# Ten products of a tile of zeros on TensorE, five ahead of and five behind the gain products, in front of the first transposes

## The chip, the cores and the metric
The kernel runs on one core of a Trainium2 chip. The metric is the device time in microseconds (us) of one execution. Before the change it is 1565.86 us, the median of three runs (1565.73 to 1567.34).

## The reference, cut to what matters
Two transformer blocks follow each other over 256 tokens of width 1024, all in float32. Only the head of the first one lies at the change:

```python
h = rmsnorm(x, norm1_w)          # x * rsqrt(mean(x*x) + eps) * gain
proj = h @ w_in                  # 1024 columns of x into retention, MoBA and gate columns
rq, rk, rv, rg, mq, mk, mv, ga, gb = split(proj)
# retention and MoBA attention, their output products, a residual,
# a gated feed-forward; then the second block of two layers (FoX and MLA
# attention, four feed-forwards, per-layer gates) on the result
```

Everything behind `proj` is the same before and after the change, and so is what is computed in the head.

## The kernel before, in words
The tokens lie in two tiles of 128 (t = 0 and 1). Each weight matrix is loaded in pieces of 128 x 2048 ("units") by SyncE's queue into a ring `w_raw`. ScalarE makes a rounded copy `w_hi` of each unit (line 1132), and VectorE, or GpSimd for some units, the rest `w_lo = w_raw - w_hi` (lines 1561 and 480). The left operand is split in the same way into `xTh` and `xTl`, and a product of float32 precision is three products of the reduced type: high by high, high by low, low by high.

The head runs as follows. GpSimd sets constants: the epsilons, `ones` (a row of 128 ones, line 462), and 128 columns of zeros in `mask[:, 0:P]` (line 463), which raises `zeros_set` to 1. ScalarE's queue loads the gain row `norm1_w` and the identity. TensorE's first work is at line 831: two products of `ones` (one row by 128 columns) by the gain row (one row by 512 columns) which spread the gain over 128 partitions into banks 2 and 3. ScalarE sums the squares of tile 0 of x, VectorE takes the reciprocal (line 1650) and multiplies x by it and by the gain from the banks (line 1661, two halves of 512 columns). TensorE transposes the result in eight products with the identity, four for each half (line 521, called from `to_xT`). ScalarE copies the two banks of transposes out as `xTh` (line 1141), and VectorE makes `xTl` (line 1601). Between the transposes of tile 0 and tile 1, TensorE runs the first products of stage `rq0`: `xTh` by `w_hi` (line 570), by `w_lo` (line 576) and `xTl` by `w_hi` (line 583), for unit 0 and then for half of unit 1.

Each engine has its instructions in a written order. ScalarE's is: squares of tile 0, `w_hi` of unit 0, the two copies of transposes of tile 0, squares of tile 1, `w_hi` of unit 1. VectorE's is: reciprocal and normalization of tile 0, `w_lo` of unit 0, the two `xTl` of tile 0, reciprocal and normalization of tile 1, `w_lo` of unit 1. TensorE's queue waits on semaphores that the others raise.

Of the kernel before, what the change touches and what calls it, by code (L numbers as in the profile page):

```python
# [30 lines left out]
P = 128  # L31
# [155 lines left out]
def build(nc, dram, marks):  # L187
# [23 lines left out]
    with ExitStack() as ctx:  # L211
        def sb(name, cols, dt=F32):
            return ctx.enter_context(nc.sbuf_tensor(name, [P, cols], dt))
# [3 lines left out]
        def sem(name):  # L217
            sems[name] = ctx.enter_context(nc.semaphore(name))
            return sems[name]
# [19 lines left out]
        mask = sb("mask", 2 * P)[:, :]  # L239
# [85 lines left out]
        bank = [low[:, b] for b in range(4)]  # L325
# [14 lines left out]
        zeros_set, rope_q_loaded = sem("zeros_set"), sem("rope_q_loaded")  # L340
# [10 lines left out]
        def mark(name, *label):  # L351

            counts[name] += 1
            if label:
                assert label not in found, label
                found[label] = (name, counts[name])
            return 1
# [34 lines left out]
        def _(sp):  # L392
# [5 lines left out]
            def load(u):  # L398
                _, kt, n, halves = units[u]
                slot = w_raw[u % RING][:, 0:kt * n].rearrange("p (k n) -> p k n", k=kt)  # L400
                if u >= RING:
                    sp.wait_ge(w_lo_done[u % RING], u // RING)
                for (k0, k1), (n0, n1), src in halves:
                    sp.dma_start(slot[:, k0:k1, n0:n1], src).then_inc(w_loaded[u % RING], 16)
# [78 lines left out]
        def gb_count(site):  # L483

            return 16 * (site + 1) if site < 2 else 32 * site
# [21 lines left out]
        def _(pe):  # L507
# [100 lines left out]
            def tile_steps(stage, banks, **kw):  # L608


                c = Chunk(stage, banks, **kw)

                def early():
                    c.run(0, tiles=(0,))
                    c.run(1, tiles=(0,), part=0)

                return [early, lambda: c.run(1, tiles=(0,), part=1), lambda: c.run(0, 1, tiles=(1,))]
# [206 lines left out]
                                   [(j * P, src[:, 2 * i + t, j * P:(j + 1) * P]) for j in range(4)])  # L824


            pe.wait_ge(ones_set, 1)
            pe.wait_ge(gb_loaded, gb_count(0))
            for q in range(2):
                take(2 + q, ("norm", 0, 1, 1))  # L830
                mm = pe.matmul(bank[2 + q], ones, gain_row[:, q * CH:(q + 1) * CH], start=True, stop=True)
            mm.then_inc(pe_done, mark("pe_done", "gain0"))
            pe.wait_ge(ident_loaded, 16)
            rq = tile_steps("rq0", (0, 1), ready=0)
            to_xT(0, normed, b0=4, between=rq[0])
# [1344 lines left out]
```

## Time and profile before
| | |
|---|---|
| median of three runs | 1565.86 us |
| the profiled execution's own time | 1565.49 us |
| its span, first to last instruction | 1563.5 us |
| mean granted TensorE clock | 0.994 of full speed |
| TensorE matmul busy | 1517.2 us, 97% of the span, 8444 instructions |
| TensorE weight load busy | 1315.5 us, 84% |
| VectorE busy | 933.9 us, 60% |
| ScalarE busy | 783.6 us, 50% |
| GpSimd busy | 182.8 us, 12% |

PE is TensorE, PEld its weight loads, DVE VectorE, ACT ScalarE, POOL GpSimd and SP SyncE. A product of full float32 operands stands as two MATMUL records and two weight loads; a transpose and a product of the reduced type as one. A record's duration holds the drain of the pipeline as well, so that back-to-back records overlap: the pace is read from start to start. "Idle before" in square brackets names what ended the wait.

### The profile page before, as it was taken

What the parts mean: (1) busy time and instruction counts of PE and PEld (TensorE: products, weight loads), DVE (VectorE), ACT (ScalarE), POOL (GpSimd) and SP (SyncE); (2) the same over time, 40 slices, a digit from 0 to 9 for tenths busy, and PEclk for the clock granted to TensorE, in tenths of its full rate; (3) what the DMA queues carried; (4) which work ended last, traced back from release to release, by engine and by line L of the source; (5) the groups of instructions that cost most, each with busy time, mean ns of one, the idle gap of its engine ahead of it and who ended that gap; (6) DMA issues with size and microseconds to landing.
All of it is one profiled execution on the core that took longest, in us unless ns stands there. A gap on an engine that the chain in (4) does not pass through costs nothing.

```text
span 1563.5 us, 22063 instructions
## 1 busy us (share of the span) xinstructions
PE 1517.2 (97%) x8444; PEld 1315.5 (84%) x8444; DVE 933.9 (60%) x1214; ACT 783.6 (50%) x935; POOL 182.8 (12%) x54
## 2 busy tenths in 40 slices
PE   8999999999999999899999999899999999999997
PEld 6888888888888888798888888788888887888885
DVE  7475465666656667214666667766666355666667
ACT  5436444444444444655454446554446554544455
POOL 0014211000010001350100002100005441100001
PEclk9999999999999999999999999999999999999999
DMA  8444345655565554532555555565554334555552
GB/s 311 168 141 170 140 162 187 216 192 188 183 193 189 189 190 159 163 134 86 175 199 188 190 193 197 171 202 190 191 192 161 103 112 164 172 199 188 188 201 81
DMA packets 186861, 274.35 MB, mean 175 GB/s; under 512 B 9953, under 2 KB 137057, under 8 KB 186722
## 3 DMA queue, kind: packets, MB, share of 16 engines
q1 hardware_dynamic: 182848, 261.72, 50.2%
q10 hardware_dynamic: 3954, 11.80, 2.3%
q8 instruction: 42, 0.69, 0.2%
q14 instruction: 17, 0.14, 0.0%
HBM read 272.44 MB, written 1.05 MB: 175 GB/s over the span
## 4 chain that ended last, share of the span: by engine, by line
PE 83%; DVE 9%; ACT 4%; issue 1%; DMA 1%; POOL 0%; ACTq 0%; SPq 0%; DVEq 0%
PE bank L652 22%; PE bank L654 12%; PE bank L525 6%; PE bank L527 6%; PE bank L526 6%; PE acc L525 6%; PE acc L526 6%; PE acc L527 6%; DVE w_lo L1561 3%; PE acc L787 2%; ACT w_hi L1132 2%; PE acc L521 2%; PE bank L576 1%; PE bank L570 1%; PE bank L583 1%
## 5 line engine op out<-in xcount | busy, mean ns | idle before, releaser
L1561 DVE TENSOR_TENSOR w_lo<-w_raw,w_hi 128x2048 fp32r<-128x2048 f32 (+2 forms) x210 | 477.1, 2276 | 181.6 <-ACT w_hi L1210 121.6
L652 PE MATMUL bank<-xT,w_hi 128*128 128x512 f32 x1520 | 380.2, 392 | 2.0 <-DVE hid L1705 1.2
L480 POOL TENSOR_TENSOR w_lo<-w_raw,w_hi 128x2048 fp32r<-128x2048 f32 (+2 forms) x42 | 176.7, 4211 | 1345.6 <-ACT w_hi L1132 1345.6
L652 PEld LDWEIGHTS bank<-xT,w_hi 128*128 128x128 f32 x1520 | 276.1, 189 | 53.9 <-DVE hid L1705 1.6
L1210 ACT ACTIVATE w_hi<-w_raw 128x2048 fp32r<-128x2048 f32 x145 | 276.5, 1907 | 0.0
L654 PEld LDWEIGHTS bank<-xT,w_lo 128*128 128x128 f32 x1520 | 207.4, 190 | 14.8
L654 PE MATMUL bank<-xT,w_lo 128*128 128x256 f32 x1520 | 211.9, 282 | 0.0
L1132 ACT ACTIVATE w_hi<-w_raw 128x2048 fp32r<-128x2048 f32 (+4 forms) x107 | 191.8, 1817 | 27.9 <-DMA w_raw<-in_w_in 7.8
L525 PE MATMUL acc<-w_hi,hTh 128*128 128x512 f32 x400 | 156.2, 391 | 0.0
L526 PE MATMUL acc<-w_lo,hTh 128*128 128x512 f32 x400 | 156.2, 391 | 0.0
L527 PE MATMUL acc<-w_hi,hTl 128*128 128x512 f32 x400 | 155.6, 389 | 0.0
L525 PE MATMUL bank<-w_hi,xT 128*128 128x512 f32 x352 | 139.7, 397 | 2.0 <-DVE w_lo L1561 1.7
L527 PE MATMUL bank<-w_hi,xT 128*128 128x512 f32 x352 | 137.3, 390 | 0.0
L526 PE MATMUL bank<-w_lo,xT 128*128 128x512 f32 x352 | 137.0, 389 | 0.0
L1220 ACT ACTIVATE squares<-bank 128x512 f32<-128x512 f32 x50 | 29.8, 597 | 140.5 <-PE bank L654 140.5
L1779 DVE CUSTOM_DVE_ANT_0 arena<-acc,mask 128x128 f32<-128x128 f32 x80 | 25.4, 355 | 121.0 <-PE acc L787 121.0
L1231 ACT ACTIVATE hTh<-hid 128x512 fp32r<-128x512 f32 x45 | 28.5, 632 | 136.2 <-PE acc L527 136.2
L527 PEld LDWEIGHTS acc<-w_hi,hTl 128*128 128x128 f32 x400 | 75.1, 188 | 16.0
L525 PEld LDWEIGHTS acc<-w_hi,hTh 128*128 128x128 f32 x400 | 75.3, 188 | 14.3
L526 PEld LDWEIGHTS acc<-w_lo,hTh 128*128 128x128 f32 x400 | 75.3, 188 | 13.7
L1220 ACT ACTIVATE tanh<-bank 128x512 f32<-128x512 f32 x45 | 26.8, 596 | 106.7 <-PE bank L654 106.7
L525 PEld LDWEIGHTS bank<-w_hi,xT 128*128 128x128 f32 x352 | 66.1, 188 | 15.9 <-DVE w_lo L1561 1.5
(221 smaller groups left out, 2145.9 us busy)
## 6 DMA issues: line engine op xcount, KB each, us to landing
w_raw<-in_ffn_w_in SPq DMA_DIRECT2D x176, 512.0 KB, 4.4
w_raw<-in_ffn_w_out SPq DMA_DIRECT2D x88, 512.0 KB, 4.2
w_raw<-in_w_in SPq DMA_DIRECT2D x52, 512.0 KB, 4.8
w_raw<-in_fox_w_in SPq DMA_DIRECT2D x24, 512.0 KB, 4.5
w_raw<-in_w_ffn_gate SPq DMA_DIRECT2D x22, 512.0 KB, 4.7
w_raw<-in_w_ffn_up SPq DMA_DIRECT2D x22, 512.0 KB, 4.5
w_raw<-in_w_ffn_down SPq DMA_DIRECT2D x22, 512.0 KB, 3.9
w_raw<-in_ple_w_gate SPq DMA_DIRECT2D x16, 512.0 KB, 4.1
```

The costliest lines, as they stand in the source:

```text
L480: pool.tensor_tensor(w_lo[s][:, 0:cols], w_raw[u % RING][:, 0:cols], w_hi[s][:, 0:cols].bitcast(F32), ALU.subtract).then_inc(w_lo_done[u % ...
L521: mm = pe.matmul(bank[b][:, c:c + P], src, ident, is_transpose=True, start=True, stop=True)
L525: pe.matmul(out, ah, bh, start=first, stop=False)
L526: pe.matmul(out, ah, bl, start=False, stop=False)
L527: return pe.matmul(out, al, bh, start=False, stop=last)
L652: pe.matmul(out, wh[:, k, m], both, start=k == 0, stop=False)
L654: mm = pe.matmul(out[:, S:], wl[:, k, m], xTh[:, k], start=False, stop=k == KD - 1)
L787: mm = pe.matmul(out if n is None else out.rearrange("p (a n) -> p a n", a=n), a, b_, start=j == 0, stop=j == len(terms) - 1)
L1132: nc.scalar.activation(w_hi[slots[u]][:, 0:cols], w_raw[u % RING][:, 0:cols], ACT.Copy)\
L1210: nc.scalar.activation(w_hi[slots[u]][:, :], w_raw[u % RING][:, :], ACT.Copy).then_inc(w_hi_done, 1)
L1220: nc.scalar.activation(dst.rearrange("p (m n) -> p m n", m=2), low[:, b:b + 2, S:], ACT.Copy)\
L1561: nc.vector.tensor_tensor(w_lo[s][:, 0:cols], w_raw[u % RING][:, 0:cols], w_hi[s][:, 0:cols].bitcast(F32), ALU.subtract).then_inc(w_lo_don ...
```

## The change
Five products of the zero tile by itself, 128 x 128 by 128 columns in float32, are issued on TensorE's queue ahead of the gain products, and five behind them, ahead of the wait for the identity. They write 128 columns of bank 0, which nothing reads before `rq0` starts that bank anew. The first batch waits for `zeros_set`. Nothing else changes.

```diff
+            pe.wait_ge(zeros_set, 1)
+            zeros = mask[:, 0:P]
+            for _ in range(5):
+                pe.matmul(bank[0][:, 0:P], zeros, zeros, start=True, stop=True)
             pe.wait_ge(ones_set, 1)
             pe.wait_ge(gb_loaded, gb_count(0))
             for q in range(2):
                 take(2 + q, ("norm", 0, 1, 1))
                 mm = pe.matmul(bank[2 + q], ones, gain_row[:, q * CH:(q + 1) * CH], start=True, stop=True)
             mm.then_inc(pe_done, mark("pe_done", "gain0"))
+            for _ in range(5):
+                pe.matmul(bank[0][:, 0:P], zeros, zeros, start=True, stop=True)
             pe.wait_ge(ident_loaded, 16)
             rq = tile_steps("rq0", (0, 1), ready=0)
             to_xT(0, normed, b0=4, between=rq[0])
```

## Rows read from the trace of the kernel before
**Rows 1.** The page: busy time by engine, and the chain's shares.
```profile
PE 1517.2 (97%) x8444; PEld 1315.5 (84%) x8444; DVE 933.9 (60%) x1214; ACT 783.6 (50%) x935; POOL 182.8 (12%) x54
PE 83%; DVE 9%; ACT 4%; issue 1%; DMA 1%; POOL 0%; ACTq 0%; SPq 0%; DVEq 0%
```
**Rows 2.** Chain that ended last, 0 to 60 us: start, us, what.
```profile
1.67 5.77 DMA w_raw<-in_w_in
...
9.41 0.51 DVE w_lo L1561
...
11.62 1.28 DVE xT L1601 x2
13.01 1.41 DVE arena L1661 x2
14.41 2.21 DVE w_lo L1561
16.67 0.73 PE bank L576 x2
```
**Rows 3.** Timeline, 0 to 30 us, TensorE: start, us, engine, line, count [idle before].
```profile
3.28 3.75 PE L831 MATMUL bank<-gb,arena 1*128 1x512 f32 x4 [3.28 <-DMA gb<-in_norm_w]
...
7.96 1.94 PE L521 MATMUL acc<-ident,arena 128*128 128x128 f32 x8 [0.93 <-DVE arena L1661]
...
10.01 2.04 PE L570 MATMUL bank<-w_hi,xT 128*128 128x512 f32 x4
...
11.85 1.62 PE L576 MATMUL bank<-w_lo,xT 128*128 128x512 f32 x4
...
13.31 1.09 PE L583 MATMUL bank<-w_hi,xT 128*128 128x512 f32 x4
...
14.69 0.61 PE L583 MATMUL bank<-w_hi,xT 128*128 128x512 f32 x2
...
16.67 0.73 PE L576 MATMUL bank<-w_lo,xT 128*128 128x512 f32 x2 [1.36 <-DVE w_lo L1561]
...
17.24 1.04 PE L521 MATMUL acc<-ident,arena 128*128 128x128 f32 x8
```
**Rows 4.** Timeline of TensorE alone, two narrow windows, 12.9 to 13.5 us.
```profile
12.35 1.12 PE L576 MATMUL bank<-w_lo,xT 128*128 128x512 f32 x3
...
12.78 0.70 PE L576 MATMUL bank<-w_lo,xT 128*128 128x512 f32 x2
```
**Rows 5.** Line 521 in 7 to 12 us: durations in ns, first and last start.
```profile
L521 PE MATMUL acc<-ident,arena x8: 421/421/447, 8.0 to 9.5; 128*128 128x128 f32 x8
```
**Rows 6.** Timeline of GpSimd, ScalarE and VectorE in the head.
```profile
0.96 0.20 POOL L463 MEMSET mask<- 128x128 f32 x1
...
1.71 1.28 ACT L1141 ACT_TABLE_LOAD   x1 [1.71 <-PEq L2169]
...
7.07 1.41 DVE L1661 SCALAR_TENSOR_TENSOR arena<-x,rstd,bank 128x512 f32<-128x512 f32 x2 [0.85 <-PE bank L831]
7.47 1.91 ACT L1132 ACTIVATE w_hi<-w_raw 128x2048 fp32r<-128x2048 f32 x1 [1.52 <-DMA w_raw<-in_w_in]
...
9.28 1.25 ACT L1141 ACTIVATE xT<-acc 128x512 fp32r<-128x512 f32 x2
...
12.01 1.90 ACT L1132 ACTIVATE w_hi<-w_raw 128x2048 fp32r<-128x2048 f32 x1
...
14.33 2.29 DVE L1561 TENSOR_TENSOR w_lo<-w_raw,w_hi 128x2048 fp32r<-128x2048 f32 x1
```
**Rows 7.** Timeline of TensorE, 1290 to 1305 us: full float32 products of 128 columns.
```profile
1290.64 0.39 PE L800 MATMUL acc<-arena 128*128 128x128 f32 x2
1290.86 0.39 PE L801 MATMUL acc<-arena 128*128 128x128 f32 x2
```
**Rows 8.** Windows of 13 us: busy time by engine, then granted clock, DMA share, GB/s.
```profile
975.00:988.00 13.00, 8.02 (x36) 6.72 (x35) 10.53 (x20) 10.73 (x16) 2.93 (x1) 0.78 0.25 81
...
1547.00:1560.00 13.00, 6.40 (x29) 4.96 (x27) 10.14 (x22) 8.59 (x13) 0.00 (x0) 0.84 0.10 40
```

## The prediction
> **What bounds the kernel now.** I read the page first, then the chain of waits for the first 60 us, then the timeline of the head engine by engine, and last the granted clock in windows over the whole span. The page shows TensorE busy for 97% of the span and carrying 83% of the chain [rows 1]. So what shortens TensorE's work shortens the kernel, wherever TensorE is what the end waits for. The change touches TensorE alone, and only before its first transposes, so the question is whether TensorE is on the chain there. The chain says it isn't. It starts with the load of the first weight unit, runs through VectorE's `w_lo` of unit 0, the two `xTl`, the normalization of tile 1 and `w_lo` of unit 1, and enters TensorE for good only at 16.67 us, at line 576 [rows 2]. In the timeline the reader sees the same from TensorE's side: it is done with all earlier work at 15.30 us (14.69 + 0.61) and idles 1.36 us until `w_lo` of unit 1 comes [rows 3].
>
> Next comes TensorE's own pace before that wait. Eight transposes take 1.94 us at 7.96 and 1.04 us at 17.24 [rows 3]. From start to start that is 0.22 us ((1.94 - 0.42) / 7, with the 0.42 us that one record lasts [rows 5]) against 0.11. A product of 512 columns starts 0.43 us after the one before (12.35 to 12.78) where later four of them take 1.09 us in all, 0.23 us each [rows 3, 4]. So the first stretch runs at half pace, the lower of the two levels of 1.2 and 2.4 GHz, although the granted-clock column has no entry below 1.00 there. Behind 12.78 two products start before the one of 13.31, so one gap was about 0.30 and the next 0.23 [rows 4]: the clock rose near 12.9 us. That is 9.6 us after TensorE's first product at 3.28, and 4.9 us after the end of its last long pause at 7.96 [rows 3].
>
> **The change, part by part.** Nothing is removed or moved; 10 products are added, which are 20 matmul records and 20 weight loads.
>
> Price of one: a full float32 product of 128 by 128 by 128 columns is in the trace of before, in the late attention. Two follow each other at 1290.64 and 1290.86, 0.22 us apart at the upper clock [rows 7]. At the lower level, where transposes and wide products both showed twice the pace, it is 0.45. Five are 1.1 us at the upper level and 2.2 at the lower. No reason excludes that a product beside a busy array costs less, but the floor is nothing; the far end is the pace of the gain products, 3.75 / 4 = 0.94 us a record [rows 3], which would make 9.4 us of five (10 records). Those stream four times the columns, so the row of equal shape is the nearest, and I take 0.45.
>
> Batch one: the zeros are there at 1.16 us (0.96 + 0.20), and another engine's start was released at 1.71 by TensorE's queue [rows 6], so TensorE can start between 1.16 and 1.7. Five cold products end at 3.4 to 3.9. TensorE was idle until 3.28, when the gain row came [rows 3]; so 2.1 us or less of the 2.2 are covered, and the gain products start 0.1 to 0.6 us late. The wait added for the zeros has the gain products queued behind it, but it is met 1.6 us or more before their row arrives.
>
> Batch two: 7.03 (3.28 + 3.75) to 7.96 was a pause of 0.93 us, in which VectorE normalized the first half [rows 3, 6]. VectorE's 7.07 hangs on the last gain product. What the five cost depends on the clock.
> (a) Clock up before or during it. In the kernel before, the clock rose 4.9 us after the end of the last pause. With the first batch in place there is no pause from 1.2 to 1.7 us on, which puts the rise at 6.1 to 6.6. By then some three of the four gain records are done; the rest goes at double pace, and the gains end near 6.9 to 7.2. Five products at 0.22 end near 8.0 to 8.3, the normalized half is there 0.9 us after the gains, 7.8 to 8.1, and the transposes start at 8.0 to 8.3. Four of them take 0.33 + 0.27 us at the upper level, so the first bank is ready at 8.6 to 8.9. ScalarE isn't: it is in `w_hi` of unit 0 until 9.38 and copies the bank at 9.28 by the record [rows 6], held by the load that landed at 7.44 [rows 2]. So nothing behind ScalarE moves.
> (b) Clock up only after it. The gains end at 7.1 to 7.6, the batch at 9.4 to 9.9, and the first bank is ready 1.08 us (3 x 0.22 + 0.42) later, at 10.5 to 11.0. ScalarE's copy moves by 1.2 to 1.7 us.
>
> What lies between the copy and the end of the head: ScalarE's order takes the copies, the squares of tile 1 and `w_hi` of unit 1, ending at 13.91 (12.01 + 1.90). VectorE takes that unit up at 14.33 [rows 6], when its own chain is through; so ScalarE has 0.4 us of slack. VectorE itself is without a gap from 9.41 to 16.62 [rows 2, 6], and its only other tie to the transposes is `xTl` at 11.62, which needs copies that end at 10.53, 1.1 us of slack. So (a) costs 0.0, and (b) costs 1.2 - 0.4 to 1.7 - 0.4, 0.8 to 1.3 us. From 16.67 on TensorE runs what it ran before, at the pace it had before.
>
> What becomes faster in (a) is real but lies in front of a wait: eight transposes save 0.9 us and the wide products from 10.01 to 12.9 save half of 2.9 us, 1.4; together 2.3 us on TensorE. They turn the idle of 1.36 us before 16.67 into one of some 2.5 to 3.6. That is the whole effect I expect to see. The cover is the DMA, ScalarE, VectorE chain; if that were shorter by x, up to x of the gain would show.
>
> The sum against the profiled execution (1565.49 us, 2.0 of it around the span of 1563.5): 0.0 in case (a). The runs' median lies 0.4 us above that execution, so the forecast stands at 1565.9 us.
>
> One rule of the Trainium skill speaks for more. The page TensorE: Matmul & The Clock Gate, section "Why this matters for your kernels", advises keeping the array busy, so that the products run at the upper level. The trace agrees that the first products here run at half pace. By that rule alone the sum would be -2.3 us, the gain at TensorE; the rows of the chain say that TensorE isn't waited for there, and that is the third case below. The same page, section "Part 4: PE-mode transpose", says that transposes don't count as work for the clock. By it the rise near 12.9 would go back to the 2.9 us of wide products from 10.01 alone, and ordinary products put in front would raise the clock sooner still: an argument for (a) and against (b). The trace can't separate the two.
>
> **The rivals.**
> First, (b), the clock doesn't rise by then: the added work doesn't do what it would have to. For it: 3.75 us of gain products without a pause didn't raise the clock, and if the time from the first product counts (9.6 us), the rise comes at 10.8 to 11.3, behind the batch. Also the gain products use one row of the array and may count for little. Against it: the stretch without a pause grows from 3.75 to over 6 us. Time: +0.8 to +1.3, 1566.7 to 1567.2. It decides once the first bank of transposes is ready later than 9.28 + 0.4; this is the case on the slow side.
> Second, TensorE does bound the head: the wait at 16.67 is really for its own earlier work, and 2.3 us come back, 1563.6 us. For it: 97% busy. Against it: the named releaser, VectorE, ended at 16.62, and TensorE was empty at 15.30.
> Third, a shift elsewhere. Late in the kernel there are stretches at a lower clock, 0.78 of 13 us at 975 and 0.84 at 1547 [rows 8]. At half pace the first is 13 x 0.22 x 2 = 5.7 us long and costs up to 2.9 us, the second up to 2.1. When such a stretch begins or ends may move with the moment at which TensorE began its work; 1 to 3 us either way, 1563 to 1569. Against it: the three runs of before lie within 1.6 us.
>
> **How the numbers follow.** (a) has 0.56, (b) 0.25, the gain in the head 0.05, a shift elsewhere 0.14. The predicted time is that of (a), 1565.9 us. The range is 1563.9 to 1568.2: above, it takes in (b) with the 1.5 us by which the highest run of before stands over the median, nearly; below, most of the shifts, and it stops just short of the second rival. The bound of 0.2% is 3.1 us, about what a measurement of this kernel can tell from no change. None of the first three cases reaches it; only a third of the shifts, or products priced at the far end, would. So 0.03 for faster, 0.92 for the same, 0.05 for slower.
>
> **What would show it.** In the profile after: 20 records of full float32 products, 10 from about 1.2 to 1.7 us on, 10 behind the gain products; the pace of the second batch (0.22 or 0.45) tells (a) from (b). Then eight transposes at 7.96 or later in 1.0 to 1.1 us rather than 1.94; ScalarE's first copy still at 9.28; VectorE's `w_lo` of unit 1 still at 14.33 to 14.41; TensorE's wait before line 576 longer than 1.36 us and still ending at 16.67. The forecast is wrong if that product starts over 0.3 us earlier or later, or if the windows behind 20 us differ in clock by more than a us's worth.

## Result: 0.3% slower, by 5.5 us, where no change was forecast

| | before | changed |
|---|---|---|
| median | 1565.63 us (22 executions) | 1571.16 us (22 executions) |
| lowest to highest | 1563.49 to 1567.84 | 1565.47 to 1575.34 |
| profiled execution, span | 1565.49, 1563.5 us | 1567.38, 1565.3 us |

The ratio is 1.0031, with a 95% interval of 1.0022 to 1.0041. The times of the changed kernel are not one cluster: 10 of the 22 lie at 1565.47 to 1568.54 us, with a median of 1566.9, and 12 at 1570.86 to 1575.34. None of the 22 of before is above 1567.84, and of all its 104 executions in this study one is above 1570 (1571.2). One more execution of before took 1887 us at a granted clock of 0.75, and is left out everywhere. The profiled execution belongs to the lower group. So its trace can show the 1.3 us by which the lower group lies above before, and not the larger loss of the other group.

The page of the changed kernel has the same balance as [rows 1], with 20 more matmul records.

```profile
PE 1521.7 (97%) x8464; PEld 1319.3 (84%) x8464; DVE 934.1 (60%) x1214; ACT 784.0 (50%) x935; POOL 182.8 (12%) x54
```

Its chain that ended last, in the head (start, us, what), to be read beside [rows 2]:

```profile
1.21 2.50 PE bank L830 x10
3.71 3.71 PE bank L835 x4
7.42 2.43 PE bank L838 x10
9.85 1.72 PE acc L521 x8
11.59 0.61 ACT xT L1147
12.28 1.16 ACT squares L1147 x2
13.76 1.81 ACT w_hi L1138
15.60 2.30 DVE w_lo L1567
17.95 0.73 PE bank L576 x2
```

Before, this chain began with a load and came to TensorE only at 16.67 us. Now it begins on TensorE at 1.21 us: the added products are what the first transposes wait for. Its timeline of TensorE, against [rows 3], shows the paces:

```profile
1.21 2.50 PE L830 MATMUL bank<-mask 128*128 128x128 f32 x10 [1.21 <-POOL mask L463]
3.64 3.78 PE L835 MATMUL bank<-gb,arena 1*128 1x512 f32 x4
7.35 2.50 PE L838 MATMUL bank<-mask 128*128 128x128 f32 x10
9.64 1.91 PE L521 MATMUL acc<-ident,arena 128*128 128x128 f32 x8
11.48 1.82 PE L570 MATMUL bank<-w_hi,xT 128*128 128x512 f32 x4
13.14 1.09 PE L576 MATMUL bank<-w_lo,xT 128*128 128x512 f32 x4
...
17.95 0.73 PE L576 MATMUL bank<-w_lo,xT 128*128 128x512 f32 x2 [1.13 <-DVE w_lo L1567]
```

Both batches take 2.50 us, eight transposes take 1.91 us as before, and four wide products still take 1.82 us at 11.48. Only the four at 13.14 take 1.09. So the clock rose near 13 us, as in the kernel before (12.9), although TensorE had been working without a pause since 1.21 us. ScalarE and VectorE, against [rows 6]:

```profile
10.74 0.60 ACT L1147 ACTIVATE xT<-acc 128x512 fp32r<-128x512 f32 x1 [1.48 <-PE acc L521]
...
13.67 1.90 ACT L1138 ACTIVATE w_hi<-w_raw 128x2048 fp32r<-128x2048 f32 x1
...
15.60 2.29 DVE L1567 TENSOR_TENSOR w_lo<-w_raw,w_hi 128x2048 fp32r<-128x2048 f32 x1 [0.20 <-ACT w_hi L1138]
```

The first copy starts at 10.74 rather than 9.28, `w_hi` of unit 1 ends 1.66 us later than before, and `w_lo` starts at 15.60 rather than 14.33. The product at the end of the head starts at 17.95 rather than 16.67: 1.28 us later.

The rest of the difference between the two profiled executions is +0.5 us (1.8 in span less 1.28). Windows of 13 us (busy time and instructions of PE, PEld, DVE, ACT and POOL, then granted clock, DMA share, GB/s) show two short stretches at a lower clock that trade places. Of the changed kernel, then of the kernel before:

```profile
169.00:182.00 13.00, 11.16 (x65) 9.45 (x64) 8.56 (x27) 9.26 (x20) 0.04 (x1) 0.87 0.24 82
```
```profile
169.00:182.00 13.00, 11.28 (x71) 10.05 (x72) 7.89 (x24) 8.21 (x16) 0.00 (x0) 1.00 0.30 106
624.00:637.00 13.00, 11.39 (x57) 8.69 (x58) 5.25 (x10) 6.12 (x7) 0.20 (x1) 0.87 0.50 163
```

Followed by ScalarE's operations, the first costs the changed kernel 1.6 us, and the second, which it doesn't have, saves it 1.6. One or the other appears in nine of the 14 traces of this study. What is left comes late in the kernel: the changed kernel makes up 0.4 us at 1200 to 1212 us and loses 0.9 us at 1344, where ScalarE takes longer over the issue of a DMA. Before, then changed:

```profile
1343.10 0.45 ACTq L1158 DMA_DIRECT2D gb<-in_ln_b  x1
```
```profile
1344.02 1.36 ACTq L1164 DMA_DIRECT2D gb<-in_ln_b  x1
```

What makes an issue long is taken up below, at the place where it costs more.

### The profile page after: what moved, and what is told of

Its sections match the earlier page's. It is cut to its first block, busy times and chain, and to the rows that moved or that the text cites. A ratio compares the mean times of both kernels' runs of the same rounds, so it can differ in the third digit from the quotient of the medians.

```text
span 1565.3 us, 22103 instructions
## 1 busy us (share of the span) xinstructions
PE 1521.7 (97%) x8464; PEld 1319.3 (84%) x8464; DVE 934.1 (60%) x1214; ACT 784.0 (50%) x935; POOL 182.8 (12%) x54
## 4 chain that ended last, share of the span: by engine, by line
PE 83%; DVE 9%; ACT 5%; issue 1%; DMA 0%; POOL 0%; ACTq 0%; DVEq 0%; SPq 0%; POOLq 0%
PE bank L652 22%; PE bank L654 12%; PE bank L525 6%; PE bank L527 6%; PE bank L526 6%; PE acc L525 6%; PE acc L526 6%; PE acc L527 6%; DVE w_lo L1567 3%; PE acc L787 2%; ACT w_hi L1138 2%; PE acc L521 2%; PE bank L576 1%; PE bank L570 1%; PE bank L583 1%
```

## Experiments

### The same kernel again: where the other group loses its time

Edit: none. The changed kernel, once more.

> The changed kernel again, unaltered. Theory H (head only): the five products behind the gain products move the head by 1.3 us in every execution, and nothing else changes; then its times stay near 1567 with the scatter of the kernel before, some 3 us. Theory C (clock elsewhere): the earlier start of TensorE also changes where in an execution the clock falls, and does so in some executions and not in others; then the times spread over 8 to 10 us again, and a trace of an execution near 1573 shows stretches of 10 us or more at the lower clock that the kernel before doesn't have.

Measured: 1568.96 us (1566.21 to 1573.63, 12 executions), ratio 1.0026 (1.0014 to 1.0038); 5 of the 12 lie above 1570. This time the profiled execution is one of them: 1572.08 us. So the times spread as they did, by more than the head alone would give. At 1204 us it is 1.75 us ahead of the first one (the operation `rsqrt_v` starts at 1204.08 rather than 1205.83), and it ends 4.9 us behind it (spans of 1570.2 and 1565.3): 6.6 us are lost between. Part of the 1.75 us is a stretch at the lower clock that this execution doesn't have (the one at 169 to 182 us of the first). Timeline there, VectorE, ScalarE and GpSimd of this execution:

```profile
1204.08 2.13 DVE L2059 TENSOR_SCALAR rsqrt_v<-stats 128x2 f32<-128x2 f32 x1 [5.93 <-ACT squares L1147]
...
1207.23 0.16 DVE L1591 TENSOR_TENSOR rsqrt_a<-rsqrt_y 128x2 f32<-128x2 f32 x1
1207.43 4.40 DVE L1593 SCALAR_TENSOR_TENSOR rsqrt_b<-rsqrt_a,rsqrt_v 128x2 f32<-128x2 f32 x1
1211.87 0.16 DVE L1595 SCALAR_TENSOR_TENSOR rsqrt_y<-rsqrt_b,rsqrt_y 128x2 f32<-128x2 f32 x1
...
1205.25 1.91 ACT L1138 ACTIVATE w_hi<-w_raw 128x2048 fp32r<-128x2048 f32 x1 [1.27 <-DMA w_raw<-in_kv_w_up]
...
1198.93 7.26 POOL L480 TENSOR_TENSOR w_lo<-w_raw,w_hi 128x2048 fp32r<-128x2048 f32 x2 [13.40 <-ACT w_hi L1138]
1207.24 4.57 POOL L480 TENSOR_TENSOR w_lo<-w_raw,w_hi 128x2048 fp32r<-128x2048 f32 x1 [1.06 <-ACT w_hi L1138]
```

And the same place in the kernel before:

```profile
1204.50 1.31 DVE L2053 TENSOR_SCALAR rsqrt_v<-stats 128x2 f32<-128x2 f32 x1 [5.90 <-ACT squares L1141]
...
1207.62 0.16 DVE L1587 SCALAR_TENSOR_TENSOR rsqrt_b<-rsqrt_a,rsqrt_v 128x2 f32<-128x2 f32 x1
...
1208.02 1.14 DVE L2057 SCALAR_TENSOR_TENSOR arena<-acc,rsqrt_y,hid 128x384 f32<-128x384 f32 x2
...
1206.63 1.92 ACT L1132 ACTIVATE w_hi<-w_raw 128x2048 fp32r<-128x2048 f32 x1 [2.24 <-DMA w_raw<-in_kv_w_up]
...
1198.54 7.25 POOL L480 TENSOR_TENSOR w_lo<-w_raw,w_hi 128x2048 fp32r<-128x2048 f32 x2 [12.55 <-ACT w_hi L1132]
1208.63 4.57 POOL L480 TENSOR_TENSOR w_lo<-w_raw,w_hi 128x2048 fp32r<-128x2048 f32 x1 [2.85 <-ACT w_hi L1132]
```

This is the reciprocal root of a normalization in the second block: twelve operations on 128 x 2 numbers. Each normally takes 0.16 us, and `arena` (the normalized rows) follows. GpSimd is at the same time making `w_lo` of the `kv_up` units, two in a row and then the fourth. In both traces `rsqrt_v` ends when GpSimd's pair does (1206.21 and 1206.19; 1205.81 and 1205.79). From there VectorE needs 2.17 us (to 1207.98) for the eleven operations behind it. Before, GpSimd was idle for 2.85 us between the pair and the fourth unit, and the operations fit. Here it was idle for 1.06 us. It starts at 1207.24, and the operation of 1207.43 ends when GpSimd does, at 1211.8: 4.40 us rather than 0.16.

TensorE's waits in 1200 to 1225 us (engine, line, releaser: us in total, times, longest) and its granted clock, both of this execution:

```profile
PE acc L1031 <- DVE arena L2063: 3.8, 1, 3.8
```
```profile
1210.00:1212.00 2.00, 0.00 (x0) 0.00 (x0) 1.97 (x2) 0.12 (x1) 1.81 (x1) 1.00 0.00 2
...
1214.00:1216.00 2.00, 0.78 (x4) 0.41 (x4) 1.12 (x2) 1.61 (x3) 0.00 (x0) 0.50 0.58 214
1216.00:1218.00 2.00, 2.00 (x9) 2.00 (x10) 0.00 (x0) 0.33 (x1) 1.60 (x1) 0.50 0.00 0
1218.00:1220.00 2.00, 2.00 (x12) 2.00 (x11) 1.57 (x4) 0.00 (x0) 1.05 (x1) 0.50 0.00 0
1220.00:1222.00 2.00, 2.00 (x16) 2.00 (x16) 0.11 (x1) 0.51 (x2) 0.00 (x0) 0.86 0.90 247
```

TensorE stands still for 3.8 us, then its clock falls to 1.2 GHz and stays there until about 1220.5. Over 1209 to 1222 us the granted clock is 0.74 where before it is 1.00. An estimate from these rows: TensorE's waits in this stretch are 5.2 us in all, where the first trace of the changed kernel has 1.6, and some 7 us at half pace cost 3.4; together 7.0, where 6.6 were lost. So the loss is about half stall and half clock.

The Trainium skill has the rule, on the page SBUF — State Buffer, section "Who interferes with whom": a VectorE instruction with two SBUF inputs contends with a GpSimd instruction that reads SBUF, and the one that comes second is blocked for the whole of the first. The trace agrees: `rsqrt_b<-rsqrt_a,rsqrt_v` has two inputs, it came 0.19 us behind GpSimd's start, and it waited for GpSimd's end.

### Which batch costs what in the head

Only the five products ahead of the gain products:
```diff
-            for _ in range(5):
-                pe.matmul(bank[0][:, 0:P], zeros, zeros, start=True, stop=True)
             pe.wait_ge(ident_loaded, 16)
```

> Only the five products ahead of the gain products. Theory H: they end at 3.7 us, so the gain products are up to 0.4 us late, which the slack in front of the first copy hides: 0.0 to +0.3 us against the kernel before, no scatter. Theory C, if what counts is the moment at which TensorE begins: the same scatter up to +10 us as in the changed kernel, median +3 to +6.

Measured: 1564.94 us (1563.45 to 1571.96, 12 executions), ratio 1.0005 (0.9991 to 1.0018). The transposes start at 8.35 rather than 7.96, and line 576 at 16.67, as before. The clock rose near 12.3 us. Three of 12 executions lie above 1570, where no scatter or a median 3 to 6 us up was expected; none of these three was traced.

Only the five behind them:
```diff
-            for _ in range(5):
-                pe.matmul(bank[0][:, 0:P], zeros, zeros, start=True, stop=True)
             pe.wait_ge(ones_set, 1)
```

> Only the five products behind the gain products. Theory H: the transposes start 1.3 us later (9.3 rather than 8.0), the head ends about 1 us later; +1 us, no scatter. Theory C, if what counts is the unbroken work before the rise: scatter up to +10 us here as well; if what counts is the first batch's early start: +1 us alone.

Measured: 1566.35 us (1563.32 to 1574.73, 11 executions), ratio 1.0014 (0.9999 to 1.0029); two lie above 1570. Line 576 starts at 17.30, 0.63 us late. That isn't the batch's doing in this execution. The gain row came 1 us earlier, the gain products started at 2.29 us, and the transposes behind the batch at 8.27. The first weight unit landed later, so that ScalarE began its `w_hi` at 8.09 rather than 7.47, 0.62 us late:

```profile
8.09 1.91 ACT L1136 ACTIVATE w_hi<-w_raw 128x2048 fp32r<-128x2048 f32 x1 [2.28 <-DMA w_raw<-in_w_in]
```

The clock rose in TensorE's pause before 10.63, but TensorE then waited 1.69 us for `w_lo` and it fell again, so that the eight transposes at 18.16 took 1.91 us rather than 1.04.

A measure that leaves the landing of the first unit out is the time from the start of that `w_hi` to line 576. It is 9.2 us in the kernel before (16.67 - 7.47) and in seven others (the small products, the late ones, the guard in the kernel before, the units moved), 9.4 with the first batch alone, 9.2 in this trace, and 10.6 in both traces of the changed kernel. So the first batch cost 0.2 us, the second nothing in an execution whose gain row came 1 us earlier, and the two together 1.4 us. Neither batch alone brings the clock up before the transposes.

The transposes held back without any added product. Three memsets on GpSimd, started behind the gain products, raise a semaphore that TensorE waits for:
```diff
+            need("pool", "gain0")
+            pool.memset(mkz[64:P, 0], 0.0).then_inc(held, 1)
...
+            pe.wait_ge(held, 3)
             pe.wait_ge(ident_loaded, 16)
```

> The kernel before with no added product; instead the first transposes wait for three memsets on GpSimd that start behind the gain products (about 2 us), so the head is late as in the changed kernel while TensorE stands idle. Theory H: +1 to +1.5 us, no scatter, as in the changed kernel. Theory C, if added activity is at fault: +1 to +1.5 us as well; if the mere shift against something in the chip is at fault: scatter up to +10 us. An idle of 2.5 us and more may also leave the clock low for longer, up to 1 us more.

Measured: 1566.41 us (1563.92 to 1572.68, 11 executions), ratio 1.0013 (1.0002 to 1.0023). Transposes start at 9.39, 1.43 us late, and line 576 at 17.74, 1.07 late (10.3 us behind `w_hi` rather than 9.2). The median is 0.8 above before's 1565.59. Late transposes alone give a loss of the head's kind, and nearly its size. Two of these 11 lie above 1570, so a loss of that size can occur without the products; those two weren't traced, and whether it is the same loss isn't shown.

### Does the collision make the upper group?

The guard: GpSimd waits, ahead of the fourth `kv_up` unit, for the normalized rows of tile 0, which end the twelve operations. It was added to both kernels:
```diff
             for u, unit in enumerate(units):
+                if u == unit_at["kv_up"][3]:
+                    need("pool", "cqn", 0)
```

> The kernel before, with one wait more on GpSimd: the rest of the fourth kv_up unit (the one that starts at 1208.6 us) may start only when VectorE has written the first half of the normalized cq, 0.1 us before it starts anyway. Theory S (the tail is a VectorE operation of 0.16 us that a GpSimd subtraction holds up for 4.4 us at this place): nothing changes in the median, 0.0 +- 0.3 us, and no execution stands 5 us or more above the median. Theory C (clock alone): no change either, so this run is the reference for the next.

Measured: 1565.45 us (1563.35 to 1567.10, 11 executions), ratio 0.9997 (0.9988 to 1.0006).

> The changed kernel with the same wait on GpSimd. Theory S: the executions near 1571 to 1575 are gone; what is left is the head's 1.3 us and the scatter of the clock, median 1566 to 1567.5, highest below 1570. Theory C (the tail comes from stretches at the lower clock alone, or from another place): about half of the executions still stand at 1571 to 1575 and the median stays at 1569 or above.

Measured: 1567.39 us (1565.81 to 1569.66, 11 executions), ratio 1.0015 (1.0006 to 1.0024). Its trace has the early pattern of the execution that collided (`rsqrt_v` takes 2.58 us), and the guard holds GpSimd until VectorE is through:

```profile
1205.26 2.58 DVE L2061 TENSOR_SCALAR rsqrt_v<-stats 128x2 f32<-128x2 f32 x1 [5.93 <-ACT squares L1149]
...
1210.05 1.14 DVE L2065 SCALAR_TENSOR_TENSOR arena<-acc,rsqrt_y,hid 128x384 f32<-128x384 f32 x2
...
1210.75 4.58 POOL L482 TENSOR_TENSOR w_lo<-w_raw,w_hi 128x2048 fp32r<-128x2048 f32 x1 [2.93 <-DVE arena L2065]
```

The unguarded changed kernel had 17 of its 34 executions above 1570 us; the guarded one has none of 11. So the collision makes the upper group, and the guard costs the kernel before nothing that can be measured. The medians of the two guarded kernels still differ by 1.9 us. The two traces don't account for it by the head: line 576 starts at 17.42 in one and 17.40 in the other. The guarded kernel of before had its first unit 0.7 us late, and in the guarded changed kernel the clock rose near 10.3 us, within the transposes, so that the time from `w_hi` to line 576 is 9.6 us rather than 10.6. In this pair ScalarE's issue at 1344 us makes some 0.6 us of difference (1.09 rather than 0.46). What makes the rest is open.

### Is it the products' work, or that there are more instructions?

The same ten products, on 16 x 16 outputs and 16 columns:
```diff
-                pe.matmul(bank[0][:, 0:P], zeros, zeros, start=True, stop=True)
+                pe.matmul(bank[0][0:16, 0:16], zeros[:, 0:16], zeros[:, 0:16], start=True, stop=True)
```

> The change with as many instructions (ten products, twenty records and twenty weight loads) but of 16 columns by 16 columns, so that the second batch costs well under 1 us and the first copy of the transposes stays within 0.5 us of 9.3. Theory F (the number of TensorE's instructions shifts where its code is fetched, and so how fast a load lands beside it late in the kernel): the tail stays as in the changed kernel, a third to a half of the executions 5 us or more above the rest. Theory D (the shift of the head in time does it): no tail and no loss, 1565.5 us.

Measured: 1571.15 us (1570.36 to 1573.46, 5 executions), ratio 1.0043 (1.0027 to 1.0060). A batch takes 0.45 us rather than 2.50, and line 576 starts at 16.64, as before. Yet every execution lies above 1570, where a third to a half was expected at most, and the traced one has the collision (4.45 us).

Ten small products in the second block, out of the head's reach:
```diff
+                if l:
+                    for _ in range(10):
+                        pe.matmul(bank[0][0:16, 0:16], mask[:, 0:16], mask[:, 0:16], start=True, stop=True)
                 if l == 0:
```

> The kernel before with ten products of 16 by 16 columns of the zeros placed late, between the last feed-forward loop ahead of the kv_up products and those products; the head is untouched. Theory F: the code behind them lies as far down as in the changed kernel, so the tail appears as in it, at a cost of 0.5 us or less otherwise. Theory D: no tail, +0.0 to +0.5 us.

Measured: 1571.20 us (1570.68 to 1573.22, 5 executions), ratio 1.0043 (1.0027 to 1.0059). VectorE, GpSimd, then TensorE's wait:

```profile
1208.21 4.51 DVE L1588 TENSOR_TENSOR rsqrt_a<-rsqrt_y 128x2 f32<-128x2 f32 x1
...
1208.15 4.56 POOL L480 TENSOR_TENSOR w_lo<-w_raw,w_hi 128x2048 fp32r<-128x2048 f32 x1 [0.99 <-ACT w_hi L1135]
```
```profile
PE acc L1028 <- DVE arena L2060: 4.0, 1, 4.0
```

The head is untouched, and the loss is whole. The same with the guard:

> The kernel before with the ten small late products (which made every execution slow, 1571.2 us) and the wait that holds GpSimd's subtraction back until VectorE has passed. Theory S (the loss is the 4.4 us hold-up and what follows it): back to 1565 to 1567, the wait is worth 4 to 6 us here though it was worth nothing in the kernel before. If the late products cost by themselves, or by another place, it stays near 1571.

Measured: 1565.47 us (1564.78 to 1566.81, 11 executions), ratio 1.0004 (0.9995 to 1.0013). And with five small products rather than ten, without the guard:

> Five small products at the late place rather than ten, no wait added: half the shift of the code. Theory F: the code fetch that lay at 1203.5 us in the kernel before and at 1196 with ten moves by some part of that; if it still falls inside the load of the fourth kv_up unit (1201 to 1206), 1565.5 us in all executions, if it falls ahead of it, 1571 in all; a mixture if it is on the edge, as in the changed kernel. A theory in which the tail grows with the number of products alone would put it at 1568 to 1569.

Measured: 1572.29 us (1571.75 to 1572.83, 5 executions), ratio 1.0049 (1.0035 to 1.0062). The loss doesn't scale with their number: it is there or not there.

### What more instructions have to do with it

Read from the 14 traces afterwards, in us. "Fetch" is the packet of queue q8, kind "instruction", nearest to the place. "Issue" is the longest of ScalarE's three DMA issues just ahead of `w_hi` of the pair. "Idle" is GpSimd's before the fourth unit.

| kernel | fetch | issue | idle | longest short operation |
|---|---|---|---|---|
| before | 1203.5 | 0.45 | 2.85 | 0.17 |
| changed | 1203.1 | 0.45 | 2.48 | 0.17 |
| changed, again | 1195.0 | 1.30 | 1.06 | 4.40 |
| only ahead | 1201.7 | 0.45 | 2.56 | 0.17 |
| only behind | 1205.8 | 0.45 | 2.94 | 0.17 |
| held back | 1203.4 | 0.45 | 3.07 | 0.17 |
| guard, before | 1204.4 | 0.45 | 2.98 (guard) | 0.17 |
| guard, changed | 1196.2 | 1.77 | 2.93 (guard) | 0.17 |
| tiny | 1194.7 | 1.51 | 0.32 | 4.45 |
| late | 1196.5 | 1.23 | 0.99 | 4.51 |
| guard, late | 1193.8 | 1.00 | 2.92 (guard) | 0.17 |
| late, five | 1195.4 | 1.64 | 0.47 | 4.42 |
| two units moved | 1200.0 | 0.45 | 3.02 | 0.17 |
| one unit moved | 1202.5 | 0.45 | 3.05 | 0.17 |

The queue's packets over the whole execution, before and with ten products more:

```profile
q8 instruction: 42, 0.69, 0.2%
```
```profile
q8 instruction: 43, 0.70, 0.2%
```

All six traces with ten products more have 43 packets, and the eight others 42, so the queue seems to bring TensorE's instructions. Two cases stand apart. In one, a packet comes 3.2 to 5.1 us after the load of the fourth `kv_up` unit is issued, and the unit's `w_hi` starts 8.0 us after that issue (before). In the other it comes 2.5 to 3.3 us ahead of the issue, at the moment in which ScalarE issues three DMAs. One of those issues then takes 1.00 to 1.77 us, which makes ScalarE, and so GpSimd's pair, late. The load in turn is through sooner: 7.08 us from issue to `w_hi` in the execution "again". Both shorten GpSimd's idle: ScalarE's delay by 0.85 (1.30 - 0.45) and the load by 0.92 (8.00 - 7.08), together 1.8, which is 2.85 - 1.06. The short operations need 2.17 us; an idle of 2.48 was enough and one of 1.06 wasn't, and nothing between was traced without the guard.

ScalarE's issue in the kernel before, and in the execution "again":

```profile
1195.51 0.45 ACTq L1158 DMA_DIRECT2D gb<-in_ln_b  x1
```
```profile
1195.05 1.30 ACTq L1164 DMA_DIRECT2D gb<-in_ln_b  x1
```

The pairing holds elsewhere in the kernel too. In the 14 traces 79 DMA issues took more than 0.9 us. 70 of them ran beside a packet of q8, although only 322 of the 7588 issues did; the other nine are all one issue at 5 to 6 us, of `head_w`. It goes with the 0.9 us that the profiled execution of the changed kernel lost at 1344: the packet came at 1344.1, with the issue of 1344.02, where before it came at 1345.5, behind it. ScalarE's issue there took 0.97 to 1.36 us in the six traces in which a packet ran beside it, and 0.45 or 0.46 in the eight others. The two places aren't tied to each other: the changed kernel's first trace has a packet beside the issue at 1344 and not at 1196, the one with five late products the other way round.

The Trainium skill, page Runtime: NRT & Kernel Launch, section "Instruction fetch mechanics", says that instructions are streamed in blocks of 16 KiB (256 instructions) over DMA, and that the cost of a block's boundary is "mostly hidden". The size agrees: 0.70 MB in 43 packets are 16 KB each. The cost is hidden for TensorE itself at this place, whose waits in 1200 to 1225 us all end with VectorE or GpSimd; what a packet does to the issues of the other queues isn't hidden.

That the collision makes the loss is shown, by the guard in two kernels. That the fetch's place makes the collision is a pairing in time in 14 traces of 14, not an experiment: nothing was run that moves the fetch and nothing else. Open, too, is why the same program has the fetch at 1203.1 in one execution and at 1195.0 in another.

### The guard, and two units moved to VectorE

The guard, and two subtractions beside which VectorE operations were held, of the first `kv_down0` unit and the second `ffn3` unit, moved from GpSimd to VectorE:
```diff
+    pool_units -= {unit_at["kv_down0"][0], unit_at["ffn3"][0] + 1}
```

> The kernel before with the wait on GpSimd, and two subtractions of GpSimd that every trace shows in VectorE's way given to VectorE: the first kv_down unit (at 970.96 us GpSimd starts it and VectorE's next operation takes 3.32 rather than 0.69 us) and the second unit of the fourth feed-forward (996.02, 4.88 us, on the chain of waits). Theory S gives -1.2 us at the first (2.6 saved, 1.45 added) and -2 us at the second (2.3 us on VectorE rather than 4.9), 1562 to 1563 in all; if VectorE is the bound at either place its gain goes, 1565.

Measured: 1563.59 us (1562.03 to 1565.29, 11 executions), ratio 0.9993 (0.9984 to 1.0002). With `kv_down0` alone:

> The same with only the first kv_down unit moved to VectorE: -1.2 us by theory S, 1564.3; it tells which of the two moves does what in the run before.

Measured: 1563.29 us (1562.13 to 1564.94, 11 executions), ratio 0.9991 (0.9982 to 1.0000). VectorE there, first in the kernel before, where `x<-x,tanh` is held beside GpSimd, then with the unit moved:

```profile
971.22 3.32 DVE L1611 SCALAR_TENSOR_TENSOR x<-x,tanh 128x512 f32<-128x512 f32 x1
```
```profile
970.93 0.69 DVE L1614 SCALAR_TENSOR_TENSOR x<-x,tanh 128x512 f32<-128x512 f32 x1
...
971.55 1.48 DVE L1564 TENSOR_TENSOR w_lo<-w_raw,w_hi 128x1280 fp32r<-128x1280 f32 x1
```

The hold-up is gone. Moving the second unit as well brought nothing more, where 2 us had been expected of it. Both are clearly faster than the changed kernel (1571.16 in its own series). Before's median in the same series is 1565.1, and neither interval lies clear below 1, so against the kernel before it stays open.

## Why the prediction was wrong

**The first batch, right.** Ten records at half pace took 2.50 us, 0.21 from start to start behind the first. What follows a batch starts 2.4 or 2.3 us after it, where 2.2 stood in the sum. The gain products started 0.36 us late (0.1 to 0.6). With that batch alone the head kept its 16.67.

**The clock, wrong; its rival, right.** The step that failed in the head: "With the first batch in place there is no pause from 1.2 to 1.7 us on, which puts the rise at 6.1 to 6.6." TensorE did work without a pause from 1.21 us, and its clock rose near 12.9. In the two other traces of the changed head it rose near 12.2 and 10.3, each time after the second batch was over at 9.64; in the seven traces with the head of before it rose between 12.3 and 15.6. So the batches may have brought the rise somewhat nearer, but not ahead of the transposes, and executions of one program differ by 2.6 us. One trace of before was too little to take the moment from. The prediction had named this against itself ("the gain products use one row of the array and may count for little") and gave it 0.25; whether that is the reason isn't shown. (b)'s numbers came in: the second batch over at 9.64 (9.4 to 9.9), the copy at 10.74 (10.5 to 11.0), the head 1.28 us late (0.8 to 1.3), with the 0.4 us of slack used up where it was found. In the trace with the rise at 10.3 the copy was at 10.58 and the head's own loss only 0.4 us (9.6 rather than 9.2 from `w_hi`), since the second bank came at the upper pace. By the 10 lower executions the whole kernel is 1.3 us slower, as (b) said; that is in part luck, since their one trace has +0.9 us at 1344 and -0.4 at 1200 to 1212 in it as well. The experiment that held the transposes back gave 1.07 in the head and 0.8 in the median, with no product in it.

**TensorE as the bound of the head, rightly dismissed.** The product at line 576 waited for `w_lo`, 1.36 us before and 1.13 after. The closest was the kernel with one unit moved, whose clock rose only near 15.6: there the wait was 0.1 us.

**A shift elsewhere, right in kind and wrong in kind of cause and size.** It was priced at 1 to 3 us and sought in the stretches of [rows 8]. The first is where it was (0.78 in both). The second is at 0.97 rather than 0.84 in the profiled execution of after, without an effect of its own that could be told. The shift that decides the result, some 6 us, lies at 1203 to 1222 us, a stretch that the prediction didn't read.

**The term that the sum lacked.** This is the step that failed for the result. "From 16.67 on TensorE runs what it ran before, at the pace it had before" says without grounds that nothing else changes. What the runs showed instead is a stall of TensorE of 3.8 us near 1210, set off by a VectorE operation held for 4.40 us, and some 7 us at half pace behind the stall. About half of the executions of the changed kernel have the loss. The added instructions were counted for their time on TensorE, and their time was nearly right. What they do as instructions wasn't asked. Small ones in the head (its timing unchanged) and small ones in the second block both brought 6 us, and the guard took away the loss of those in the second block. By what path more instructions do it, the fetch, is supported by pairing alone. The trace of before showed the site: a 0.65 us margin between the last short operation's end (1207.98) and GpSimd's start (1208.63), and other VectorE operations held for 3 us beside GpSimd. In the changed kernel's own profiled execution the margin was 0.28 (1209.55 - 1209.27). A look for VectorE's operations far over their usual length would have found the neighbours of this one, and with it a stall of some 4 us; that half pace follows for some 7 us, the trace of before doesn't show.

## What to carry to other kernels

Before calling a small edit free, look in the profile for places that hold by a few tenths of a microsecond, above all short VectorE operations with two SBUF inputs beside a long GpSimd operation. Instructions added elsewhere can tip one: ten in the head and ten in the second block did. An explicit wait at the place cost nothing here and took away 3.8 us of the median in one kernel and 5.7 in the other. When executions of one kernel fall into two groups, profile one of each before explaining the median. And products put in front to raise TensorE's clock pay only if it does rise before what waits behind them, and if TensorE is what is waited for there.

## What the runs showed of the hardware that was not expected

TensorE worked without a pause from 1.21 us, first a batch of 128-row products, then one-row products, then a second batch, and its clock was still low at 9.64 in three traces of three. It rose near 12.9, 12.2 and 10.3. Which of the rows of work count can't be told from these runs.

A VectorE operation of 0.16 us took 4.40 to 4.51 beside one GpSimd subtraction, and an operation with one tensor input, `rsqrt_v<-stats`, was held as well, until GpSimd's pair ended.

A DMA issue on ScalarE's queue took 1.00 to 1.77 us rather than 0.45 in all six executions in which an instruction packet came at that moment, and in none of the eight others. Of all issues over 0.9 us behind the first 10 us of the kernel, every one, 70 of 70, ran beside such a packet.

TensorE stalls of 3.8 to 4.0 us came with some 7 us at 1.2 GHz behind them in all four traces that have them (0.74 over 1209 to 1222 us). The ten others have only one wait of 1.5 to 2.2 us and at most a shorter one of 0.7 in that stretch: seven kept the clock there (1.00), and three, with waits of 2.1 or 2.2 us, had a short stretch at the lower clock (0.87 to 0.89). The kernel before waited 2.0 us and kept it.
